# Cached keys of the differential attention loaded in 32 by 32 blocks and transposed by VectorE

## The chip, the cores and the metric

One core of one Trainium2 chip runs the whole step as one launch. The metric is the device time of one execution in microseconds (us). The core has TensorE (matrix products and full transposes through an identity matrix), VectorE, ScalarE, GpSimd and SyncE (SP), which issues most of the DMAs; 16 DMA engines carry them.

## The reference

One step of an encoder layer for two groups of requests that share the weights: a prompt of 1024 rows, and 8 running streams of 16 new rows each with 1024 cached rows. The layer has three branches (a recurrence, a differential attention, an attention over memory), a merge and a feed-forward part, all in fp32. The change touches only the scores of the running streams against their cached keys in the differential attention, which has 8 heads; a row of a cached key holds two keys of 64 values:

```python
def _diff_attention(q, k, v, pos_q, pos_k, rel_bias, lam):
    B, H, Lk, _ = k.shape
    k = k.reshape(B, H, Lk, 2, DIFF_DH)
    logits = jnp.einsum('bhqmd,bhkmd->bhmqk', q, k).astype(jnp.float32) * DIFF_SCALE
    logits = logits + _t5_bias(rel_bias, pos_q, pos_k)[None, :, None]
    p = jax.nn.softmax(jnp.where(visible, logits, -jnp.inf), axis=-1)
    w = p[:, :, 0] - lam * p[:, :, 1]
    return jnp.einsum('bhqk,bhkv->bhqv', w.astype(v.dtype), v)
```

`k` and `v` of a stream are the 1024 cached rows followed by its 16 new ones.

## The kernel before

The kernel runs phase by phase; `diff_phase` is the third. It loops over the heads, and each engine has its own instruction stream (`head(i)` in each block). A head has two parts. The prompt part goes over 8 blocks of 128 queries: scores `S0` to `S7`, their maximum on VectorE (`row_max`), the exponential on ScalarE (`probs`), the difference of the two maps on VectorE (`join`, which writes the weights), and a transpose of the weights with the product by the values (`T0` to `T8`) on TensorE. The sample part takes the 8 streams in two groups of 4: their cached keys must stand with the features on the partitions (`KT0` to `KT7`), then come the scores `SL0`, `SL1`, the maximum (`sample_max`), the exponential (`sample_probs`), the transposed weights (`PT0`, `PT1`) and the product by the cached values (`OS0`, `OS1`).

The names in the list `R` are results in PSUM, in the order in which TensorE makes them. They go in turn to two halves of PSUM, so a result waits until the last but one has been read (`take`, `freed`); `wait_freed` makes an engine wait until a result has been read. Twelve of them carry a rider: a third of one of the four projections (q, k, v, gate) that the next head or the end of this head needs, 24 matmuls that stand ahead of the result's own work in the same `take`, read by ScalarE in `finish`. The three gate riders go into the buffer `gt` ("diff_gate"). The weights of the riders are loaded by SP two at a time into a double buffer, rounded by ScalarE (`round_w`, line 108) and reduced to their rest by GpSimd (line 113). In a head ScalarE rounds the value weights right after `T0`, for all heads but the last.

The keys of a stream are 1024 rows of 128 values. One DMA (line 866) brings them with 128 rows on the partitions, 8 pieces of 512 bytes each. TensorE transposes the 8 tiles (line 1230) into PSUM, and ScalarE (line 974, even streams) or VectorE (line 1097, odd streams) copies them into `pb`, the buffer that holds the prompt's probabilities before, one place for each of 4 streams. There are four landing buffers: three of `cached_k`, and as slot 3 the gate's buffer, free between the store of one head's gate and the first gate rider of the same head's sample part. `kslot` says which stream goes to which buffer and in which turn.

SP issues in order, on one queue: the last head's gate and y stores, four key loads, four value loads (line 869), the value and gate weights, the stores of new keys and values, the next q and k weights, the prompt bias, the key loads 4 to 7 as buffers come free, value loads 4 to 7 after `OS0`, and the sample bias.

Of the kernel before, what the change touches and what calls it, by code (L numbers as in the profile page):

```python
# [14 lines left out]
P = 128  # L15
# [716 lines left out]
def diff_phase(g):  # L732
# [37 lines left out]
        "diff_consts_in", "bias_row_out", "bias_in", "bias_tables_ready", "bias_tables_out", "lambda_products",  # L770
        "lambda_exp", "diff_zeroed", "pool_turn"))

    kslot = ((0, 0), (1, 0), (3, 0), (2, 0), (0, 1), (1, 1), (2, 1), (0, 2))
    kbuf = [kc[:, 0], kc[:, 1], kc[:, 2], gt[:, 0:PAST].rearrange("p (t n) -> p t n", n=P)]
    kuses = [sum(n == slot for n, _ in kslot) for slot in range(len(kbuf))]
    kc_in, vc_in = [g.sem(f"cached_k{n}_in") for n in range(len(kbuf))], [g.sem(f"cached_v{n}_in") for n in range(4)]
    hbp_in, hbs_in = g.sem("head_bias_prompt_in"), g.sem("head_bias_sample_in")
    out_k, out_v, out_y, out_gt = (g.sem(n) for n in ("diff_k_out", "diff_v_out", "y1_out", "diff_gate_out"))
    (over_r, nm_r, w_r, sq_r, ln_r, rs_r, y_r, gt_r) = (g.sem(n) for n in (
# [5 lines left out]
    before = Results(g, ["Q", "BR", "K", "V"])  # L785
    g.r += before.n
    R = Results(g, ["S0", "VT", "S1", "KR", "S2", "T0", "S3", "T1", "S4", "T2", "S5", "T3", "S6", "T4", "S7", "T5",
                    "T6", "T7", "KT0", "T8", "KT1", "KT2", "KT3", "SL0", "KT4", "KT5", "KT6", "KT7", "PT0", "SL1",
                    "OS0", "PT1", "G", "OS1", "OC", "MS"])
    assert R.n % 2 == 0  # L790

    riders = dict(zip(("VT", "KR", "T0", "T1", "T2", "T3", "T4", "T5", "T6", "KT4", "G", "MS"),
                      [(p, c) for p in range(4) for c in range(NC)]))
    Q_LAST, K_LAST = "T0", "T3"

# [2 lines left out]
        return n in riders and not (last and riders[n][0] < 3)  # L798

    def bank(n):  # L800
        return 3 if n in ("VT", "KR", "MS") else 2

    def keys(t):

# [5 lines left out]
    with nc.Block() as block:  # L810
        @block.sync
        def _(sp):
# [47 lines left out]
            def load_k(i, b):  # L860
                slot, turn = kslot[b]
                if turn:
                    sp.wait_ge(g.full, R.full_value(f"KT{kslot.index((slot, turn - 1))}", i))
                if slot == 3:
                    sp.wait_ge(out_gt, i * 16 + 16)
                sp.dma_start(kbuf[slot], cached(kd, i, b)).then_inc(kc_in[slot], 16)

            def load_v(i, b):
                sp.dma_start(vc[:, b % 4], cached(vd, i, b)).then_inc(vc_in[b % 4], 16)
# [48 lines left out]
        def _(act):  # L918
# [11 lines left out]
            def head(i, last=False):  # L930
                def result(n):
                    return R.ready(act, n, i)

                def rider_out(n):

                    p, c = riders[n]

                    buf, scale = ((qn, DH ** -0.5), (kn, 1.0), (vt, 1.0), (gt, 1.0))[p]
                    if n == "T4":
                        act.wait_ge(out_k, i * 32 + 64)  # L940
                    elif n == "KT4":
                        act.wait_ge(out_gt, i * 16 + 16)
                    ins = act.activation(buf[:, c * CW:(c + 1) * CW], R.ready(act, n, i)[:, bank(n), 0:CW],
                                         ACT.Copy, scale=scale)
                    return ins
# [23 lines left out]
                        ins = act.activation(ot[:, (t - 1) * P:t * P], ps[:, 3, 0:P], ACT.Copy)  # L969
                    finish(f"T{t}", ins)  # L970

                def cached_kt(b):
                    ps = result(f"KT{b}")
                    finish(f"KT{b}", act.activation(pb[:, b % 4, 0:PAST], flat(ps[:, 0:2, :]), ACT.Copy))

                def sample_probs(n):
                    ps = flat(result(f"SL{n}"))
                    act.wait_ge(nm_r, i * 10 + (NQ + n + 1))
# [2 lines left out]

                def sample_turned(n):
                    ps = result(f"PT{n}")
                    R.freed(act.activation(tiles(wt[:, n, :]), ps[:, 0:NC, 0:CW], ACT.Copy), f"PT{n}")
                probs(0)
                ps = result("VT")
                act.wait_ge(out_v, i * 32 + 32)
# [11 lines left out]
                if not last:  # L999
                    g.round_w(act, first + 4, i, NW)  # L1000
                turned(NQ - 1)
                cached_kt(0)
                turned(NQ)
                cached_kt(2)
                act.wait_ge(y_r, i + 1)
                R.wait_freed(act, "T8", i)
                act.activation(sq[:, 0:SEQ], ot[:, 0:SEQ], ACT.Square)
                sample_probs(0)
                cached_kt(4)
                cached_kt(6)  # L1010
                sample_turned(0)
                sample_probs(1)
                sample_turned(1)
# [20 lines left out]
        def _(dve):  # L1034
# [33 lines left out]
            def head(i):  # L1068
                def result(n):
                    return R.ready(dve, n, i)  # L1070

                def row_max(t):
                    ps = result(f"S{t}").rearrange("p (m a) n -> p m (a n)", m=2)
                    near = slice(max(t - 1, 0) * P, keys(t))
                    w = near.stop - near.start
                    bias = hbp[:, 2 * P - w:2 * P].unsqueeze(1).to_broadcast([P, 2, w])
                    if t == 0:
                        dve.wait_ge(hbp_in, i * 16 + 16)
                    g.dve.done(dve.tensor_tensor(ps[:, :, near], ps[:, :, near], bias, ALU.add))
                    g.dve.done(dve.tensor_reduce(nm[:, t % 2, :], ps[:, :, 0:keys(t)], AX.X, ALU.max))  # L1080
                    dve.tensor_scalar(nm[:, t % 2, :], nm[:, t % 2, :], -1.0, None, ALU.mult).then_inc(nm_r, 1)

                def join(t):

                    a, b = pb[:, 2 * (t % 2), 0:keys(t)], pb[:, 2 * (t % 2) + 1, 0:keys(t)]
                    R.wait_freed(dve, f"S{t}", i)
                    g.dve.done(dve.reciprocal(cf[:, t % 2, :], sm[:, t % 2, :]))
                    g.dve.done(dve.tensor_scalar(cf[:, t % 2, 1:2], cf[:, t % 2, 1:2], nlam[:], None, ALU.mult))
                    g.dve.done(dve.tensor_scalar(a, a, cf[:, t % 2, 0:1], None, ALU.mult))
                    if t >= 2:  # L1090
                        dve.wait_ge(g.full, R.full_value(f"T{t - 2}", i))
                    dve.scalar_tensor_tensor(wb[:, t % 2, 0:keys(t)], b, cf[:, t % 2, 1:2], a, ALU.mult, ALU.add)\
                        .then_inc(w_r, 1)

                def cached_kt(b):
                    ps = result(f"KT{b}")
                    R.freed(dve.tensor_copy(pb[:, b % 4, 0:PAST], flat(ps[:, 0:2, :])), f"KT{b}")

                def sample_max(n):
                    ps = flat(result(f"SL{n}"))  # L1100
                    near = ps[:, PAST - P:ROWS]
                    g.dve.done(dve.tensor_tensor(near, near, hbs[:, n, :], ALU.add))
                    g.dve.done(dve.tensor_reduce(nm[:, n, 0:1], ps[:, 0:ROWS], AX.X, ALU.max))
                    dve.tensor_scalar(nm[:, n, 0:1], nm[:, n, 0:1], -1.0, None, ALU.mult).then_inc(nm_r, 1)

                def sample_factor(n):
                    R.wait_freed(dve, f"SL{n}", i)
                    g.dve.done(dve.reciprocal(cf[:, n, 0:1], sm[:, n, 0:1]))
                    g.dve.done(dve.tensor_tensor(cf[:, n, 0:1], cf[:, n, 0:1], sgn[:], ALU.mult))

                def sample_rows(n):

                    ps = result(f"OS{n}")
                    R.freed(dve.tensor_scalar(orow[:, n, :], ps[:, 0, 0:P], cf[:, n, 0:1], None, ALU.mult), f"OS{n}")
                row_max(0)
                row_max(1)
                for t in range(NQ):
                    join(t)
                    if t < NQ - 2:
                        row_max(t + 2)  # L1120
                cached_kt(1)
                cached_kt(3)
                dve.wait_ge(hbs_in, i * 16 + 16)
                sample_max(0)
                cached_kt(5)
                sample_factor(0)
                cached_kt(7)
                sample_max(1)
                sample_rows(0)
                sample_factor(1)  # L1130
                sample_rows(1)
                dve.wait_ge(rs_r, i + 1)
                dve.scalar_tensor_tensor(ot[:], ot[:], subl[:], sq[:], ALU.mult, ALU.mult).then_inc(y_r, 1)
# [45 lines left out]
        def _(pe):  # L1179
# [9 lines left out]
            def head(i, last=False):  # L1189
# [32 lines left out]
                                            stop=(n == t - 1))  # L1222
                    ins.then_inc(g.full, 1)

                def cached_kt(b):
                    ps, _ = take(f"KT{b}")
                    slot, turn = kslot[b]
                    pe.wait_ge(kc_in[slot], i * (16 * kuses[slot]) + 16 * (turn + 1))
                    for n in range(PAST // P):
                        ins = pe.transpose(ps[:, n // 4, (n % 4) * P:(n % 4 + 1) * P], kbuf[slot][:, n, :], g.ident[:])  # L1230
                    ins.then_inc(g.full, 1)

                def sample_scores(n):
                    ps, _ = take(f"SL{n}")
                    for b in (0, 1, 2, 3):
                        R.wait_freed(pe, f"KT{4 * n + b}", i)
                        rows = slice(b * 32, (b + 1) * 32)
                        for a in range(2):
                            pe.matmul(ps[rows, a, :], qb[:, 4 * n + b, :], pb[:, b, a * 512:(a + 1) * 512],
# [29 lines left out]
                    turn(t - 2)  # L1269
                turn(NQ - 2)  # L1270
                turn(NQ - 1)
                cached_kt(0)
                turn(NQ)
                for b in range(1, 4):
                    cached_kt(b)
                sample_scores(0)
                for b in range(4, DEC_B):
                    cached_kt(b)
                sample_turn(0)
                sample_scores(1)  # L1280
                sample_out(0)
# [1164 lines left out]
```

## Time and profile before

| | us |
|---|---|
| median of 3 runs | 3757.93 (3755.12 to 3761.45) |
| profiled execution, from first to last instruction (its span) | 3746.6 |
| TensorE matmuls busy | 3425.0 (91%) |
| VectorE busy | 1326.0 (35%) |
| ScalarE busy | 1170.4 (31%) |
| the DMA queue of SP, share of the 16 engines | 26.4% |

The profile gives the span of the profiled execution and no other time of it; the runs are timed with what lies before the first and after the last instruction, and their median is 11.3 us above the span. A wait is put down to what released it last. Times in the rows are counted from the start of the span.

### The profile page before, as it was taken

The numbers are of one execution on the slowest core, as the hardware profiler recorded it, in microseconds if no ns is written. First come the engines' busy times: TensorE is split into PE (matmuls) and PEld (weight loads), VectorE is DVE, ScalarE is ACT, GpSimd is POOL, SyncE is SP. The second block draws the span as 40 slices with busy tenths as digits, with TensorE's granted clock in tenths as the row PEclk, the third lists the DMA queues.
The fourth block names the chain that finished last, engine by engine and source line by source line (L and its number), as shares of the span: only waits on it lengthen the run. The fifth ranks groups of instructions, "written<-read, shape, count | busy, mean of one in ns | idle before, by whom it ended". The sixth has DMA issues, their size and how long they took to land. (4 is left out here: it accounts for less than half of the span.)

```text
span 3746.6 us, 51117 instructions
## 1 busy us (share of the span) xinstructions
PE 3425.0 (91%) x20480; PEld 3145.2 (84%) x20480; DVE 1326.0 (35%) x1424; ACT 1170.4 (31%) x1585; POOL 892.0 (24%) x522
## 2 busy tenths in 40 slices
PE   6999999999868999889968998899989999999997
PEld 5988899888857777777758887899988988888986
DVE  6344443453142343333431212122214443343443
ACT  4323333234223434433433222111223222222222
POOL 3233322332210111111101111124334222222220
PEclk8999999999989999999979998899989999999998
DMA  3111111011254244442444332543212111111101
GB/s 103 54 34 59 52 59 59 29 59 53 58 149 135 69 115 122 123 117 74 116 113 139 103 99 91 193 139 103 72 46 64 38 39 44 37 37 39 39 22 61
DMA packets 425088, 295.58 MB, mean 79 GB/s; under 512 B 17140, under 2 KB 405780, under 8 KB 425024
## 3 DMA queue, kind: packets, MB, share of 16 engines
q1 hardware_dynamic: 421616, 287.45, 26.4%
q10 hardware_dynamic: 3408, 7.22, 0.5%
q8 instruction: 47, 0.77, 0.1%
q14 instruction: 17, 0.14, 0.0%
HBM read 240.23 MB, written 54.41 MB: 79 GB/s over the span
## 5 line engine op out<-in xcount | busy, mean ns | idle before, releaser
L113 POOL TENSOR_TENSOR weight_lo<-weight_stage,weight_hi 128x1024 fp32r<-128x1024 f32 x180 | 436.1, 2423 | 1930.2 <-ACT weight_hi L108 1930.2
L160 PE MATMUL group<-h_hi_part,weight_hi 128*128 128x384 f32 x1608 | 581.2, 361 | 118.7 <-DVE key_rows L569 61.6
L161 PE MATMUL group<-h_lo_part,weight_hi 128*128 128x384 f32 x1608 | 558.4, 347 | 0.0
L162 PE MATMUL group<-h_hi_part,weight_lo 128*128 128x384 f32 x1608 | 557.5, 347 | 0.0
L160 PEld LDWEIGHTS group<-h_hi_part,weight_hi 128*128 128x128 f32 x1608 | 317.2, 197 | 155.5 <-issue 64.5
L1652 PE MATMUL group<-act_hi_part,weight_hi 128*128 128x512 f32 (+1 forms) x1056 | 378.0, 358 | 13.5 <-DVE act_lo_part L1880 9.1
L1654 PE MATMUL group<-act_hi_part,weight_lo 128*128 128x512 f32 (+1 forms) x1056 | 376.5, 357 | 0.0
L1653 PE MATMUL group<-act_lo_part,weight_hi 128*128 128x512 f32 (+1 forms) x1056 | 373.8, 354 | 0.0
L108 ACT ACTIVATE weight_hi<-weight_stage 128x1024 fp32r<-128x1024 f32 x180 | 190.7, 1060 | 497.4 <-PE group L1922 231.9
L161 PEld LDWEIGHTS group<-h_lo_part,weight_hi 128*128 128x128 f32 x1608 | 316.5, 197 | 1.9 <-issue 1.9
L162 PEld LDWEIGHTS group<-h_hi_part,weight_lo 128*128 128x128 f32 x1608 | 315.8, 196 | 0.0
L1920 PE MATMUL group<-act_hi_part,weight_hi 128*128 128x384 f32 x768 | 260.0, 339 | 11.3 <-DVE act_lo_part L1833 11.3
L1921 PE MATMUL group<-act_lo_part,weight_hi 128*128 128x384 f32 x768 | 259.0, 337 | 0.0
L1922 PE MATMUL group<-act_hi_part,weight_lo 128*128 128x384 f32 x768 | 259.0, 337 | 0.0
L1652 PEld LDWEIGHTS group<-act_hi_part,weight_hi 128*128 128x128 f32 x1056 | 200.2, 190 | 45.5 <-issue 9.7
L1654 PEld LDWEIGHTS group<-act_hi_part,weight_lo 128*128 128x128 f32 x1056 | 201.6, 191 | 32.8
L1653 PEld LDWEIGHTS group<-act_lo_part,weight_hi 128*128 128x128 f32 x1056 | 200.7, 190 | 32.6
L2168 DVE TENSOR_TENSOR residual<-residual,group 128x1152 f32<-128x1152 f32 x88 | 119.2, 1354 | 194.6 <-PE group L2257 194.6
L2255 PE MATMUL group<-ffn_hi_part,down_hi 128*128 128x384 f32 x528 | 178.9, 339 | 5.9 <-DVE ffn_lo_part L2163 5.9
L145 PE MATMUL group<-h_hi_part,weight_hi 128*128 128x384 f32 x504 | 173.9, 345 | 6.1 <-PEq L217 5.6
L2256 PE MATMUL group<-ffn_lo_part,down_hi 128*128 128x384 f32 x528 | 178.1, 337 | 0.0
L2257 PE MATMUL group<-ffn_hi_part,down_lo 128*128 128x384 f32 x528 | 178.0, 337 | 0.0
(328 smaller groups left out, 6160.7 us busy)
## 6 DMA issues: line engine op xcount, KB each, us to landing
weight_stage<-in_w_in SPq DMA_DIRECT2D x88, 512.0 KB, 4.1
cached_v<-in_cache_diff_v SPq DMA_DIRECT2D x64, 512.0 KB, 7.2
cached_k<-in_cache_diff_k SPq DMA_DIRECT2D x56, 512.0 KB, 4.1
weight_stage<-in_w_up SPq DMA_DIRECT2D x44, 512.0 KB, 3.7
y_stage<-scratch_y_branch SPq DMA_DIRECT2D x24, 576.0 KB, 9.8
gate_in<-scratch_gates SPq DMA_DIRECT2D x24, 576.0 KB, 3.7
weight_stage<-in_w_branch SPq DMA_DIRECT2D x24, 512.0 KB, 3.8
down_stage<-in_w_down SPq DMA_DIRECT2D x22, 512.0 KB, 3.6
```

The costliest lines, as they stand in the source:

```text
L108: act.activation(self.whi[:, n % 2, :], self.wst[:, n % 2, :], ACT.Copy).then_inc(self.w_hi, 1)
L113: pool.tensor_tensor(self.wlo[:, n % 2, :], self.wst[:, n % 2, :], self.whi[:, n % 2, :].bitcast(F32), ALU.subtract).then_inc(self.w_lo, 1)
L160: pe.matmul(out, wh[:, k, :], xh[:, k, cols], start=(k == 0), stop=False)
L161: pe.matmul(out, wh[:, k, :], xl[:, k, cols], start=False, stop=False)
L162: last = pe.matmul(out, wl[:, k, :], xh[:, k, cols], start=False, stop=(k == KT - 1))
L1652: pe.matmul(o, w[0][:, k, :], ahi[:, k, rows], start=(k == 0), stop=False)
L1653: pe.matmul(o, w[0][:, k, :], alo[:, k, rows], start=False, stop=False)
L1654: last = pe.matmul(o, w[1][:, k, :], ahi[:, k, rows], start=False, stop=(k == KT - 1))
L1920: pe.matmul(o, wh[:, k, :], ahi[:, k, cols], start=(k == 0 and open_sum), stop=False)
L1921: pe.matmul(o, wh[:, k, :], alo[:, k, cols], start=False, stop=False)
L1922: last = pe.matmul(o, wl[:, k, :], ahi[:, k, cols], start=False, stop=(k == KT - 1))
L2255: pe.matmul(o, dhi[:, f, cols], fhi[:, f, rows], start=(f == 0), stop=False)
```

## The change

The four landing buffers are used flat, as 128 by 1024. A stream's keys come in four DMAs, one for each 32 features: partition 32q + r gets, for each of 32 groups j of 32 rows, the 32 values 32q to 32q + 31 of row 32j + r. One instruction of VectorE then transposes all blocks of 32 by 32 and writes the keys into `pb`. The eight results `KT0` to `KT7`, their transposes on TensorE and their copies are gone, and the semaphore `cached_k_turned` takes their place for TensorE and SP. Stream 0 now uses slot 3, the gate's buffer. The rider that stood on `KT4` stands on `PT0`. VectorE turns streams 0 to 3 after the last `join` and streams 4 to 7 after the maximum of `SL0`.

```diff
-    kslot = ((0, 0), (1, 0), (3, 0), (2, 0), (0, 1), (1, 1), (2, 1), (0, 2))
-    kbuf = [kc[:, 0], kc[:, 1], kc[:, 2], gt[:, 0:PAST].rearrange("p (t n) -> p t n", n=P)]
+    kslot = ((3, 0), (0, 0), (1, 0), (2, 0), (0, 1), (1, 1), (2, 1), (0, 2))
+    kbuf = [flat(kc[:, 0]), flat(kc[:, 1]), flat(kc[:, 2]), gt[:, 0:PAST]]
...
-                    "T6", "T7", "KT0", "T8", "KT1", "KT2", "KT3", "SL0", "KT4", "KT5", "KT6", "KT7", "PT0", "SL1",
-                    "OS0", "PT1", "G", "OS1", "OC", "MS"])
+                    "T6", "T7", "T8", "SL0", "PT0", "SL1", "OS0", "PT1", "G", "OS1", "OC", "MS"])
...
@@ SP
             def load_k(i, b):
                 slot, turn = kslot[b]
                 if turn:
-                    sp.wait_ge(g.full, R.full_value(f"KT{kslot.index((slot, turn - 1))}", i))
+                    sp.wait_ge(kt_r, i * DEC_B + (kslot.index((slot, turn - 1)) + 1))
                 if slot == 3:
                     sp.wait_ge(out_gt, i * 16 + 16)
-                sp.dma_start(kbuf[slot], cached(kd, i, b)).then_inc(kc_in[slot], 16)
+                blocks = kd[b, ds(i, 1)].rearrange("h (j r) d -> r (h j) d", r=32)
+                for q in range(P // 32):
+                    sp.dma_start(kbuf[slot][q * 32:(q + 1) * 32, :].rearrange("r (j c) -> r j c", c=32),
+                                 blocks[:, :, q * 32:(q + 1) * 32]).then_inc(kc_in[slot], 16)
@@ ScalarE: the copies of KT0, KT2, KT4, KT6 go, and the gate rider waits for stream 0's transpose
-                    elif n == "KT4":
+                    elif n == "PT0":
                         act.wait_ge(out_gt, i * 16 + 16)
+                        act.wait_ge(kt_r, i * DEC_B + 1)
@@ VectorE
                 def cached_kt(b):
-                    ps = result(f"KT{b}")
-                    R.freed(dve.tensor_copy(pb[:, b % 4, 0:PAST], flat(ps[:, 0:2, :])), f"KT{b}")
+                    slot, turn = kslot[b]
+                    dve.wait_ge(kc_in[slot], i * (64 * kuses[slot]) + 64 * (turn + 1))
+                    if b < 4:
+                        dve.wait_ge(w_r, i * NQ + (NQ - 1 + b // 2))
+                    else:
+                        dve.wait_ge(g.full, R.full_value("SL0", i))
+                    dve.transpose(pb[:, b % 4, 0:PAST], kbuf[slot]).then_inc(kt_r, 1)
...
-                cached_kt(1)
-                cached_kt(3)
+                for b in range(4):
+                    cached_kt(b)
                 dve.wait_ge(hbs_in, i * 16 + 16)
                 sample_max(0)
-                cached_kt(5)
+                for b in range(4, DEC_B):
+                    cached_kt(b)
                 sample_factor(0)
-                cached_kt(7)
                 sample_max(1)
@@ TensorE: cached_kt and its calls go
                     for b in (0, 1, 2, 3):
-                        R.wait_freed(pe, f"KT{4 * n + b}", i)
+                        pe.wait_ge(kt_r, i * DEC_B + (4 * n + b + 1))
```

## Rows read from the trace of the kernel before

**Rows 1.** The page: the span, TensorE's total, the key loads (last column: landing).
```profile
span 3746.6 us, 51117 instructions
PE 3425.0 (91%) x20480; PEld 3145.2 (84%) x20480; DVE 1326.0 (35%) x1424; ACT 1170.4 (31%) x1585; POOL 892.0 (24%) x522
...
cached_k<-in_cache_diff_k SPq DMA_DIRECT2D x56, 512.0 KB, 4.1
```

**Rows 2.** TensorE's waits, 1060 to 2015 us: for whom, total, times, longest.
```profile
PE group L1206 <- ACT probs L957: 53.2, 20, 9.5
PE group L1230 <- DMA cached_k<-in_cache_diff_k: 12.3, 8, 1.7
```

**Rows 3.** What the weight rounding (line 108) waited for, 1060 to 2015 us.
```profile
  DMA weight_stage<-in_w_in: 35.1, 7
```

**Rows 4.** ScalarE's timeline: start, duration, instruction, [idle before it, releaser]; two heads.
```profile
1085.29 1.06 ACT L108 ACTIVATE weight_hi<-weight_stage 128x1024 fp32r<-128x1024 f32 x1 [12.18 <-DMA weight_stage<-in_w_in]
1101.22 0.91 ACT L957 ACTIVATE probs<-group,row_max 128x768 f32<-128x768 f32 x1 [3.28 <-DVE row_max L1081]
...
1446.69 1.06 ACT L108 ACTIVATE weight_hi<-weight_stage 128x1024 fp32r<-128x1024 f32 x1 [2.98 <-DMA weight_stage<-in_w_in]
1460.07 0.91 ACT L957 ACTIVATE probs<-group,row_max 128x768 f32<-128x768 f32 x1 [3.28 <-DVE row_max L1081]
```

**Rows 5.** TensorE's timeline: scores S4 of head 0, S1 and S4 of the other head.
```profile
1087.74 2.51 PE L1206 MATMUL group<-diff_k,diff_q 64*128 64x512 f32 x8 [9.46 <-ACT probs L957]
...
1427.38 0.84 PE L1206 MATMUL group<-diff_k,diff_q 64*128 64x256 f32 x4 [2.53 <-ACT probs L957]
...
1449.14 1.36 PE L1206 MATMUL group<-diff_k,diff_q 64*128 64x512 f32 x8 [0.26 <-ACT probs L957]
```

**Rows 6.** SP's timeline at the start of one head's loads.
```profile
1425.38 0.37 SPq L901 DMA_DIRECT2D scratch_gates<-diff_gate  x1
...
1427.00 1.88 SPq L866 DMA_DIRECT2D cached_k<-in_cache_diff_k  x2
...
1439.52 3.48 SPq L102 DMA_DIRECT2D weight_stage<-in_w_in  x2
```

**Rows 7.** The DMA view, 1430 to 1450 us: packets, bytes, rate.
```profile
DMA packets 11891, 5.99 MB, mean 300 GB/s; under 512 B 187, under 2 KB 11891, under 8 KB 11891
```

**Rows 8.** The DMA view, 4 to 5 us: loads of single fp32 values.
```profile
DMA packets 2152, 0.05 MB, mean 47 GB/s; under 512 B 2076, under 2 KB 2152, under 8 KB 2152
```

**Rows 9.** The DMA view, 1038 to 1041 us: bias loads into 16 partitions each.
```profile
DMA packets 1337, 0.32 MB, mean 108 GB/s; under 512 B 786, under 2 KB 1337, under 8 KB 1337
```

**Rows 10.** Windows: length, busy time of the five engines, granted clock, DMA share, GB/s.
```profile
1430.00:1432.00 2.00, 2.00 (x8) 2.00 (x7) 0.85 (x3) 0.95 (x4) 0.00 (x0) 0.50 1.15 327
```

**Rows 11.** VectorE's timeline in the same head: last `join`, first sample maximum.
```profile
1478.90 0.76 DVE L1089 TENSOR_SCALAR probs<-probs,row_factor 128x1024 f32<-128x1024 f32 x1
1479.88 1.28 DVE L1092 SCALAR_TENSOR_TENSOR weights<-probs,row_factor 128x1024 f32<-128x1024 f32 x1 [0.22 <-DVE probs L1089]
...
1498.32 0.43 DVE L1102 TENSOR_TENSOR group<-group,head_bias_sample 128x256 f32<-128x256 f32 x1 [2.42 <-PE group L1241]
```

**Rows 12.** TensorE's timeline, T8 (1489.34), SL0 (1494.58), KT4 to KT7, SL1 (1509.75).
```profile
1489.34 2.02 PE L1221 MATMUL group<-weights_t,diff_v_rows 128*128 128x128 f32 x16 [0.50 <-ACT diff_out L969]
...
1494.58 3.29 PE L1239 MATMUL group<-probs,query_blocks 128*32 128x512 f32 x16
1497.80 0.49 PE L1241 MATMUL group<-diff_k,query_blocks 128*128 128x128 f32 x2
1502.29 1.91 PE L1230 MATMUL group<-ident,cached_k 128*128 128x128 f32 x16
...
1509.75 1.95 PE L1239 MATMUL group<-probs,query_blocks 128*32 128x512 f32 x16 [0.34 <-DVE probs L1097]
1511.63 0.49 PE L1241 MATMUL group<-diff_k,query_blocks 128*128 128x128 f32 x2
```

**Rows 13.** ScalarE's timeline, the exponential of SL0.
```profile
1500.37 1.23 ACT L979 ACTIVATE weights<-group,row_max 128x1152 f32<-128x1152 f32 x1 [5.26 <-DVE row_max L1104]
```

More of the change, by code:

```diff
@@ L771, in diff_phase @@
         "lambda_exp", "diff_zeroed", "pool_turn"))
-    kslot = ((0, 0), (1, 0), (3, 0), (2, 0), (0, 1), (1, 1), (2, 1), (0, 2))
-    kbuf = [kc[:, 0], kc[:, 1], kc[:, 2], gt[:, 0:PAST].rearrange("p (t n) -> p t n", n=P)]
+    kslot = ((3, 0), (0, 0), (1, 0), (2, 0), (0, 1), (1, 1), (2, 1), (0, 2))
+    kbuf = [flat(kc[:, 0]), flat(kc[:, 1]), flat(kc[:, 2]), gt[:, 0:PAST]]
     kuses = [sum(n == slot for n, _ in kslot) for slot in range(len(kbuf))]
     kc_in, vc_in = [g.sem(f"cached_k{n}_in") for n in range(len(kbuf))], [g.sem(f"cached_v{n}_in") for n in range(4)]
+    kt_r = g.sem("cached_k_turned")
     hbp_in, hbs_in = g.sem("head_bias_prompt_in"), g.sem("head_bias_sample_in")
@@ L787, in diff_phase @@
     R = Results(g, ["S0", "VT", "S1", "KR", "S2", "T0", "S3", "T1", "S4", "T2", "S5", "T3", "S6", "T4", "S7", "T5",
-                    "T6", "T7", "KT0", "T8", "KT1", "KT2", "KT3", "SL0", "KT4", "KT5", "KT6", "KT7", "PT0", "SL1",
-                    "OS0", "PT1", "G", "OS1", "OC", "MS"])
+                    "T6", "T7", "T8", "SL0", "PT0", "SL1", "OS0", "PT1", "G", "OS1", "OC", "MS"])
     assert R.n % 2 == 0
-    riders = dict(zip(("VT", "KR", "T0", "T1", "T2", "T3", "T4", "T5", "T6", "KT4", "G", "MS"),
+    riders = dict(zip(("VT", "KR", "T0", "T1", "T2", "T3", "T4", "T5", "T6", "PT0", "G", "MS"),
                       [(p, c) for p in range(4) for c in range(NC)]))
@@ L800, in bank @@
     def bank(n):
-        return 3 if n in ("VT", "KR", "MS") else 2
+        return 3 if n in ("VT", "KR", "PT0", "MS") else 2
     def keys(t):
@@ L970, in turned @@
                     finish(f"T{t}", ins)
-                def cached_kt(b):
-                    ps = result(f"KT{b}")
-                    finish(f"KT{b}", act.activation(pb[:, b % 4, 0:PAST], flat(ps[:, 0:2, :]), ACT.Copy))
                 def sample_probs(n):
@@ L983, in sample_turned @@
                     ps = result(f"PT{n}")
-                    R.freed(act.activation(tiles(wt[:, n, :]), ps[:, 0:NC, 0:CW], ACT.Copy), f"PT{n}")
+                    finish(f"PT{n}", act.activation(tiles(wt[:, n, :]), ps[:, 0:NC, 0:CW], ACT.Copy))
                 probs(0)
@@ L1001, in head @@
                 turned(NQ - 1)
-                cached_kt(0)
                 turned(NQ)
-                cached_kt(2)
                 act.wait_ge(y_r, i + 1)
@@ L1008, in head @@
                 sample_probs(0)
-                cached_kt(4)
-                cached_kt(6)
                 sample_turned(0)
@@ L1095, in cached_kt @@
                 def cached_kt(b):
-                    ps = result(f"KT{b}")
-                    R.freed(dve.tensor_copy(pb[:, b % 4, 0:PAST], flat(ps[:, 0:2, :])), f"KT{b}")
+                    slot, turn = kslot[b]
[5 more added lines that the diff above has]
+                    dve.transpose(pb[:, b % 4, 0:PAST], kbuf[slot]).then_inc(kt_r, 1)
                 def sample_max(n):
@@ L1223, in turn @@
                     ins.then_inc(g.full, 1)
[L1225 to L1231, printed above, removed]
                 def sample_scores(n):
@@ L1271, in head @@
                 turn(NQ - 1)
-                cached_kt(0)
                 turn(NQ)
-                for b in range(1, 4):
-                    cached_kt(b)
                 sample_scores(0)
-                for b in range(4, DEC_B):
-                    cached_kt(b)
                 sample_turn(0)
```

## The prediction

> **What bounds the kernel now.** I read the totals first, then who waits for whom in the stage of the change, then one head by engine, then the DMA queue. TensorE is busy for 91% of the span [rows 1], so an instruction taken off it counts almost in full, unless the time goes into a wait. The eight heads of the differential attention lie between about 1060 and 2015 us, near 119 us each; the head shown begins its loads at 1427.00 and ends its sample part near 1530. Two waits of TensorE matter in them: for ScalarE's `probs` (53.2 us in 20 waits) and for the cached keys (12.3 us in 8) [rows 2].
>
> The first has a cause one step further back. In seven heads ScalarE rounds the next value weights right after T0, and stands still for their landing: 35.1 us in 7 waits [rows 3]; 12.18 us in head 0, 2.98 us in the head shown [rows 4]. TensorE then waits for the `probs` behind that rounding: 9.46 us in head 0, 0.26 us in the head shown [rows 5], so 2.7 us of delay are covered and every further one reaches TensorE in full. What it waits for is a queue: SP issues the gate and y stores, four key loads, four value loads, then the weights at 1439.52 [rows 6], and from 1430 to 1450 the DMA engines never rest (300 GB/s [rows 7], a busy share of 1.15 in its first 2 us [rows 10]). **Whatever makes the four key loads longer makes each of these seven waits longer**, one for one. The landing is on the path already.
>
> **The loads.** Per head, 8 key loads of 1024 packets of 512 B become 8 groups of four DMAs with 4096 packets of 128 B in all; the bytes stay. 11891 packets in 20 us are 16 x 20000 / 11891 = 26.9 ns for one packet on one engine, 64 of them 1.72 us a load; by bytes (512 KB at 300 GB/s) 1.75 us, which I use [rows 7]. No row has 128 B packets. Below lies the column load of 4 B packets: 2076 in 1 us, 7.7 ns each [rows 8]; above, 26.9 ns if a packet of 128 B costs what one of 512 B does. A straight line between them gives 7.7 + 124/508 x 19.2 = 12.4 ns, and 256 x 12.4 = 3.2 us a load. The new DMAs write 32 partitions each. Where the kernel loads its bias with DMAs into 16 partitions, the queue moved 0.32 MB in 3 us, 108 GB/s [rows 9]; if that is a limit of the partitions, 32 have twice as much, 2.4 us a load. I take 3.4 us, the line and a little for the crowding; the ends are 2.0 (7.7 ns) and 6.9 us (26.9 ns).
>
> The Trainium skill, page "DMA: Bandwidth & Descriptors", section "Why small descriptors are slow (HBM only)", puts a fixed cost of about 3 cycles on each packet beside one for every 32 B. That would make a 128 B packet cost 7/19 of a 512 B one, an estimate of 10.1 ns and 2.6 us a load; by the sum below that is 3749 us, a little faster than now.
>
> Four loads of a head stand before the weights: 4 x (3.4 - 1.75) = 6.6 us. The first load of a head now goes to slot 3, the gate's buffer, and waits for the gate store; the first load was issued at 1427.00 and this one can go about 1428.3 (the store issued at 1425.38, some 2.9 us to landing), but the y store still fills the engines then, so I put 0.5 us (0 to 1.3) on it. SP issues 12 more instructions for the four loads at 0.35 to 0.4 us, inside the time of the transfers. So the weights land 7.1 us later in seven heads: 50 us. The last head rounds nothing after T0 and pays nothing.
>
> A long wait also costs TensorE its clock. After 9.46 us of waiting in head 0, ScalarE's `probs` of 768 keys came 1101.22 - 1085.29 = 15.9 us behind the rounding's start, against 1460.07 - 1446.69 = 13.4 us in the head shown [rows 4]: 2.5 us. In the head shown TensorE waits 2.53 us at 1427.38 [rows 5], and from 1430 to 1432 the granted clock is 0.50, the lower of its two levels (1.2 and 2.4 GHz) [rows 10]. Six heads now join head 0: 15 us. Cost in front: 65 us.
>
> **The tail of a head.** Gone from TensorE are 64 transposes a head in groups of 8 at about 1.04 us, 8.3 us, with the waits between them. ScalarE and VectorE lose four PSUM copies each. VectorE gains eight transposes of 128 x 1024. Not in the trace; the nearest rows of that length are 0.76 us (probs scaled in SBUF) and 1.28 us (the join of two) [rows 11]; I take 1.25 us, and 2.5 us as the worse end. The first four start when the last join ends, at 1481.2, and take until 1486.2, or 1491.2 at the worse end; T8 ends at 1491.4 [rows 12], so they are covered either way. Their price if they were not is 1.25 us each.
>
> The two sample scores decide. SL0 could start at 1494.58, and stretched to 3.29 us waiting for the copy of key 3; now it starts at 1491.4, runs 1.95 us as SL1 does, and with its last matmuls is done at 1493.8, not 1498.3 [rows 12]. From there TensorE must wait, because the gate product that filled this gap rides on PT0 behind the exponentials: VectorE's maximum takes from 1498.32 to 1500.2 and ScalarE's exponential 1.23 us and a read [rows 11, 13], so TensorE idles 3.5 us, to 1497.3. The product takes 4.1 us (1498.2 to 1502.3 before), PT0's transposes 1.15: 1502.5. SL1 needs the eighth key, whose buffer is free only when key 4 is transposed: 1493.8 + 1.9 + 1.25 = 1497.0. Its load took 4.1 us to land [rows 1], now 4.1 + 1.65 = 5.75, so 1502.9, transposed 1504.2, and SL1 ends at 1505.2 against 1512.1: 6.9 us earlier. All waits of the keys are in that. If the clock falls in the 3.5 us of idling, the product takes some 2.7 us more and SL1 ends at 1507.6: 4.5 us. The half clock of rows 10 came after a gap of 2.53 us, other gaps went without, so I give this an even chance and take 5.5 us; eight heads give 44 us.
>
> **Sum.** +50 +15 -44 = +21 us. On the span of 3746.6 us this is 3768; the runs' median is 11.3 us above the span (stretches before and after it that the change leaves alone), so 3757.9 + 21 = **3779 us**, 0.6% slower. Every 0.1 us a load moves it by 2.8 us.
>
> **Rivals.** A, faster: the small packets are cheap, at the partition bound of 2.4 us a load. The wait in front grows by 4 x 0.65 + 0.5 = 3.1 us, 22 us in seven heads, 8 for the clock, and the tail gives 48: 3740, and 3730 to 3750 around it. It decides below about 2.65 us a load. For it: 4 B packets pass at 7.7 ns, so little of a packet's cost needs to be fixed. Against: between the two sizes that the trace shows, the line asks for more. The skill's estimate above falls to this side.
>
> B, no change: 2.65 to 2.85 us a load, 3751 to 3765; the two terms then cancel.
>
> C, much slower: a 128 B packet costs nearly what a 512 B one does, 5 to 6.9 us. At 6.9 the landing is 21 us late in seven heads (148 us), 15 us for the clock, and keys 4 to 6, requested near 1484, are in at 1506, so the eighth lands at 1513 and the tail loses 3 us a head instead of gaining: 3945. At 5 us it is 3835 to 3840. For it: no row has such packets from HBM into SBUF in number. The Trainium skill, same page, "Specifications", says that below 512 B a transfer is no longer at line rate, since a read-modify-write is done; the 4 B row does not bear out a heavy price.
>
> D, VectorE's transposes take 2.5 us or more: SL1 comes 2.5 us later, 20 us in all on top of the forecast, 3799. It decides only once eight of them no longer fit the 10 us before SL0. Against: a pass over 1024 values takes 1.28 us.
>
> **Chances.** Forecast (2.85 to 4.2 us a load, D's case with it) 0.50, its own range 3765 to 3805; A 0.22, B 0.13, C 0.15. The range that leaves out 2 in 10 cuts the far end of C and the lowest of A: 3738 to 3850. This kernel's measurement tells about 0.2% (7.5 us) from no change; below 3750.4 lies A, within it B: faster 0.22, same 0.13, slower 0.65.
>
> **What would show it.** ScalarE's wait for the weights: from 35 us in seven heads to about 85; 35 to 60 speaks for A or B, over 130 for C. TensorE's wait for `probs` grows with it. The granted clock of the stretch behind T1 falls to 0.50 in all seven heads. The DMA window of the head's start shows packets of 128 B at 12 to 14 ns. VectorE's transpose row reads near 1.25 us, and its wait for key 7 is the last before SL1. I am wrong if the packets' cost is off by more than 0.8 us a load, or if the sample part ends no earlier.

## The result, and the profile after

The changed kernel took 3770.09 us (median of 4 runs, 3767.17 to 3774.05) against 3756.52 us before (4 runs, 3751.8 to 3761.45): ratio 1.004, 95% interval 1.0025 to 1.0054. The change costs 0.4%; 3779 us was forecast. The profiled execution has a span of 3765.2 us, 18.6 us above that of before. That is more than the 13.6 us between the medians. The section on the time before put the 11.3 us between median and span down to what lies before and after the instructions; the changed kernel's executions show only 1.9 to 3.0 us of that (3767.17 us for the span of 3765.2). So the profiled execution of before was itself some 8 us faster than its median.

The page after, then TensorE's waits in the stage (for whom, total, times, longest) and ScalarE's waits at the rounding; [rows 1 to 3] have them before:

```profile
span 3765.2 us, 50542 instructions
PE 3381.5 (90%) x19968; PEld 3113.5 (83%) x19968; DVE 1362.1 (36%) x1456; ACT 1139.0 (30%) x1553; POOL 892.7 (24%) x522
...
cached_k<-in_cache_diff_k SPq DMA_DIRECT2D x224, 128.0 KB, 4.2
```

```profile
PE group L1207 <- ACT probs L961: 104.6, 20, 16.0
PE group L160 <- ACT weights L979: 28.2, 8, 3.5
PE group L1222 <- ACT diff_out L973: 10.3, 8, 1.4
```

```profile
  DMA weight_stage<-in_w_in: 88.1, 7
```

TensorE is busy 43.5 us less and the kernel is slower: the saved work went into waits. ScalarE stands 88.1 us for the weights instead of 35.1, and TensorE 104.6 us for the `probs` behind it instead of 53.2 [rows 2, 3]. Two heads in ScalarE's timeline, and TensorE's scores S4 behind the rounding ([rows 4, 5] before):

```profile
1091.21 1.06 ACT L108 ACTIVATE weight_hi<-weight_stage 128x1024 fp32r<-128x1024 f32 x1 [18.68 <-DMA weight_stage<-in_w_in]
...
1214.05 1.06 ACT L108 ACTIVATE weight_hi<-weight_stage 128x1024 fp32r<-128x1024 f32 x1 [12.05 <-DMA weight_stage<-in_w_in]
```

```profile
1093.65 2.51 PE L1207 MATMUL group<-diff_k,diff_q 64*128 64x512 f32 x8 [15.96 <-ACT probs L961]
1216.49 2.51 PE L1207 MATMUL group<-diff_k,diff_q 64*128 64x512 f32 x8 [9.33 <-ACT probs L961]
```

Over the seven heads TensorE's waits at S4 add up to 69.0 us, against 16.1 before: +53.0 us. The DMA view during the key loads of heads 1 and 2:

```profile
DMA packets 12107, 1.53 MB, mean 139 GB/s; under 512 B 12107, under 2 KB 12107, under 8 KB 12107
...
DMA packets 13730, 1.74 MB, mean 145 GB/s; under 512 B 13706, under 2 KB 13730, under 8 KB 13730
```

The first is 1192 to 1203 us, 16 x 11000 / 12107 = 14.5 ns for one 128 B packet on one engine; the second 1314 to 1326 us, 14.0 ns. A load so takes 3.6 to 3.7 us where it took 1.75.

The tail of head 1 on TensorE (T8, SL0, the gate product from 1265.97, PT0, SL1, the first matmuls of OS0), and on VectorE ([rows 11, 12] before):

```profile
1258.10 2.05 PE L1222 MATMUL group<-weights_t,diff_v_rows 128*128 128x128 f32 x16 [1.28 <-ACT diff_out L973]
1260.08 1.94 PE L1232 MATMUL group<-probs,query_blocks 128*32 128x512 f32 x16
1261.96 0.49 PE L1234 MATMUL group<-diff_k,query_blocks 128*128 128x128 f32 x2
1265.97 0.44 PE L160 MATMUL group<-h_hi_part,weight_hi 128*128 128x384 f32 x1 [3.52 <-ACT weights L979]
1271.83 1.15 PE L179 MATMUL group<-ident,weights 128*128 128x128 f32 x9
1272.90 1.95 PE L1232 MATMUL group<-probs,query_blocks 128*32 128x512 f32 x16
1274.78 0.49 PE L1234 MATMUL group<-diff_k,query_blocks 128*128 128x128 f32 x2
```

```profile
1249.94 1.24 DVE L1098 STREAM_TRANSPOSE probs<-diff_gate 128x1024 f32<-128x1024 f32 x1
1251.10 3.46 DVE L1098 STREAM_TRANSPOSE probs<-cached_k 128x1024 f32<-128x1024 f32 x3
...
1264.51 3.50 DVE L1098 STREAM_TRANSPOSE probs<-cached_k 128x1024 f32<-128x1024 f32 x3
1271.21 1.25 DVE L1098 STREAM_TRANSPOSE probs<-cached_k 128x1024 f32<-128x1024 f32 x1 [3.20 <-DMA cached_k<-in_cache_diff_k]
```

SL0 comes right behind T8 and takes 1.94 us, TensorE idles 3.52 us in all eight heads (28.2 us above), and the gate product takes 5.86 us (1265.97 to 1271.83) where it took 4.25 (1498.04 to 1502.29), since the clock falls within it: its matmuls take 0.34 us each, from 1267.75 to 1270.63 0.52, and 0.34 again. In six heads it takes 5.8 to 5.9 us, in the other two 6.67 and 7.08. The windows (length, five engines' busy time, granted clock, DMA share, GB/s) of the stretch behind S4 and of the gate product both show 0.50, the lower of the two levels. The third line is the stretch behind S4 of the same head before. Behind S4 the clock is 0.50 in all seven heads after, in head 0 alone before.

```profile
1216.00:1219.00 3.00, 2.51 (x9) 1.27 (x9) 0.00 (x0) 1.26 (x5) 1.53 (x1) 0.50 0.80 239
...
1268.00:1270.00 2.00, 2.00 (x8) 2.00 (x8) 0.01 (x1) 0.00 (x0) 0.00 (x0) 0.50 1.28 172
...
1210.00:1213.00 3.00, 2.47 (x16) 1.70 (x15) 0.72 (x2) 1.60 (x7) 1.87 (x1) 1.00 1.05 318
```

What the lower clock costs shows from the start of S4 to the product of T7, which holds the same work in both kernels. T7's product in head 1 after, then in the head shown before (S4 at 1216.49 and 1449.14):

```profile
1254.99 1.83 PE L1222 MATMUL group<-weights_t,diff_v_rows 128*128 128x128 f32 x14 [0.69 <-ACT next_v L947]
...
1486.14 1.83 PE L1221 MATMUL group<-weights_t,diff_v_rows 128*128 128x128 f32 x14 [0.68 <-ACT next_v L943]
```

That is 38.5 us against 37.0. Over the seven heads it adds up to 272.2 us after and 261.5 before: +10.7 us.

From T8 to the first product of OS0 it is 17.3 us here, 22.9 in the head shown before (1489.34 to 1512.27). Summed over the eight heads, 141.8 us against 184.3: -42.5 us. So the 18.6 us of the two spans are +53.0 at the weights, +10.7 from S4 to T7, -42.5 in the tails, -6.8 in the rest of the stage (3.7 of it in the last head before T8) and +4.2 behind the stage, in code that is the same. No run shows a cause for the last term; it is about as large as the 5.0 us by which the spans differ more than the medians.

### The profile page after: what moved, and what is told of

Its sections match the earlier page's. It is cut to its first block and busy times, and to the rows that moved or that the text cites. A ratio compares the mean times of both kernels' runs of the same rounds, so it can differ in the third digit from the quotient of the medians.

```text
span 3765.2 us, 50542 instructions
## 1 busy us (share of the span) xinstructions
PE 3381.5 (90%) x19968; PEld 3113.5 (83%) x19968; DVE 1362.1 (36%) x1456; ACT 1139.0 (30%) x1553; POOL 892.7 (24%) x522
## 5 line engine op out<-in xcount | busy, mean ns | idle before, releaser
L160 PE MATMUL group<-h_hi_part,weight_hi 128*128 128x384 f32 x1608 | 590.8, 367 | 147.4 <-DVE key_rows L569 61.6
L161 PE MATMUL group<-h_lo_part,weight_hi 128*128 128x384 f32 x1608 | 567.1, 353 | 0.0
L162 PE MATMUL group<-h_hi_part,weight_lo 128*128 128x384 f32 x1608 | 566.4, 352 | 0.0
L1640 PE MATMUL group<-act_hi_part,weight_hi 128*128 128x512 f32 (+1 forms) x1056 | 378.5, 358 | 13.5 <-DVE act_lo_part L1868 9.1
L1207 PE MATMUL group<-diff_k,diff_q 64*128 64x512 f32 (+3 forms) x384 | 93.0, 595 | 106.2 <-ACT probs L961 106.2
L145 PE MATMUL group<-h_hi_part,weight_hi 128*128 128x384 f32 x504 | 174.5, 346 | 6.1 <-PEq L217 5.6
```

Of the source, the lines that this page charges most:

```text
L160: pe.matmul(out, wh[:, k, :], xh[:, k, cols], start=(k == 0), stop=False)
L161: pe.matmul(out, wh[:, k, :], xl[:, k, cols], start=False, stop=False)
L162: last = pe.matmul(out, wl[:, k, :], xh[:, k, cols], start=False, stop=(k == KT - 1))
L1640: pe.matmul(o, w[0][:, k, :], ahi[:, k, rows], start=(k == 0), stop=False)
```

## The experiments

The kernel before was run beside each group of experiments; its medians were 3753.35 us (e1 to e4), 3751.86 (e5 to e8) and 3750.69 (e9 to e11). So kernels are compared by their ratio to it, where the changed kernel has 1.004.

### e1 and e2: the weights issued ahead of the keys

The same move in both kernels:

```diff
+                g.load_w(sp, following[0], first + 2, i, NW)
+                if not last:
+                    g.load_w(sp, following[1], first + 3, i, NW)
                 for b in range(4):
                     load_k(i, b)
                 for b in range(4):
                     load_v(i, b)
-                g.load_w(sp, following[0], first + 2, i, NW)
-                if not last:
-                    g.load_w(sp, following[1], first + 3, i, NW)
```

> The changed kernel with one move on SP: the value and gate weights are issued before the four key loads of a head, not behind the value loads. My theory (the key packets cost time only because the weights stand behind them in the queue): ScalarE's 88 us of waits for the weights go, TensorE's waits behind the rounding (15.96 us in head 0, near 9 us in six heads, about 70 us) go, and with them 7 x 2.5 us of low clock: 3770 - 87 = 3683 us. The first four keys land 3.5 us later and stay covered. Rival (the seven waits are not the price; the loss is spread, in contention of the DMA engines or in the tail): less than half of it comes back, over 3725 us.

> The kernel before with the same move. My theory: its 35 us of waits for the weights hold 16 us of waits of TensorE and one fall of the clock (2.5 us): 3756 - 18 = 3738 us. With e1 this shows what the change is worth once the queue is out of the way: about 55 us. Rival (the gate product's new gap and the clock eat the saved transposes): e1 is no better than e2.

e1: 3681.38 us (3678.48 to 3688.88), ratio 0.9811 (0.9788 to 0.9834), 2.3% below the changed kernel, some 86 us; 87 were expected. ScalarE waits for weights no more, and S4 to T7 adds up to 259.0 us, so the waits are worth 69.0 us and the clock 13.2. e2: 3731.05 us (3730.25 to 3734.72), ratio 0.9944 (0.9924 to 0.9963), 22 us below the kernel before; 18 were expected. TensorE's two longest waits in the stage, in e1, then in e2:

```profile
PE group L1207 <- ACT probs L961: 35.9, 13, 6.9
PE group L160 <- ACT weights L979: 28.2, 8, 3.5
```

```profile
PE group L1206 <- ACT probs L957: 36.2, 13, 6.9
PE group L1230 <- DMA cached_k<-in_cache_diff_k: 12.2, 8, 1.6
```

The waits for `probs` are now equal, 13 in place of 20: the seven at S4 are gone in both. So in the changed kernel the key packets cost time through the queue in front of the weights, and with that out of the way the change is worth 1.3% (0.9811 against 0.9944), about 50 us. Once the weights go first, the packets show in the tail too (e8). The rival that the new gap eats the saved transposes falls.

### e3: the changed kernel with rows of 512 B

```diff
-                blocks = kd[b, ds(i, 1)].rearrange("h (j r) d -> r (h j) d", r=32)
-                for q in range(P // 32):
-                    sp.dma_start(kbuf[slot][q * 32:(q + 1) * 32, :].rearrange("r (j c) -> r j c", c=32),
-                                 blocks[:, :, q * 32:(q + 1) * 32]).then_inc(kc_in[slot], 16)
+                sp.dma_start(kbuf[slot].rearrange("p (t n) -> p t n", n=P), cached(kd, i, b)).then_inc(kc_in[slot], 64)
```

> The changed kernel with each key load as one DMA of rows of 512 B, as before; VectorE transposes what is there, so the scores of the cached keys are of wrongly arranged keys. My theory: the waits for the weights fall from 88 back to about 35 us, and the saving of the tail stays (5.5 us a head, and key 7 lands 1.5 us earlier): 3700 to 3712 us. Rival (the four transposes more on VectorE, or slot 3 first, hold part of the loss): it stays above 3730 us.

3708.24 us (3704.46 to 3713.27), ratio 0.9885 (0.9865 to 0.9905). ScalarE's waits at the rounding are back at what they were in [rows 3]:

```profile
  DMA weight_stage<-in_w_in: 36.3, 7
```

VectorE transposes keys that are wrongly arranged here, so this is a probe and no kernel to use. All else of the change is in, and it is 45 us faster than before. The gain of the tail is real, and the whole loss is in how the keys are fetched.

### e4: the kernel before with 128 B packets

TensorE's wait for the keys counts four DMAs here (not shown):

```diff
-                sp.dma_start(kbuf[slot], cached(kd, i, b)).then_inc(kc_in[slot], 16)
+                for q in range(P // 32):
+                    cols = slice(q * 32, (q + 1) * 32)
+                    sp.dma_start(kbuf[slot][:, :, cols], cached(kd, i, b)[:, :, cols]).then_inc(kc_in[slot], 16)
```

> The kernel before with each key load cut into four DMAs of 32 features, over all 128 partitions: 128 B packets, and all else as it was. My theory (a packet of 128 B costs 14 ns whatever the partitions): each load takes 3.6 us instead of 1.75, the weights land 7.5 us later in seven heads (53 us), 15 us of clock, and key 7 lands 1.9 us later in eight heads (15 us): 3756 + 83 = 3839 us. Rival (the 32 partitions of one DMA are what made the loads long, the packets alone take 2.6 us): 3756 + 24 + 10 + 7 = 3797 us or less.

3833.72 us (3829.33 to 3838.12), ratio 1.0211 (1.0189 to 1.0233): 80 us slower, 83 expected. The waits at the rounding, and the DMA view from 1069 to 1078 us (14.6 ns a packet):

```profile
  DMA weight_stage<-in_w_in: 84.1, 7
```

```profile
DMA packets 9861, 1.26 MB, mean 140 GB/s; under 512 B 9860, under 2 KB 9860, under 8 KB 9860
```

Packets of 128 B alone, with TensorE still transposing, bring the waits. The waits at S4 grow from 16.1 to 65.0 us, S4 to T7 from 261.5 to 274.6, and the tails from 184.3 to 200.2: 78 of the 80 us. Here each DMA goes to all 128 partitions, so the packet price does not come from the 32.

### e5 and e6: packet size and number of partitions, taken apart

Both leave the keys wrongly arranged for the block transposes. e5 writes 128 B packets over 128 partitions, e6 packets of 512 B into 32. Each replaces the four lines of the change that issue the DMAs (not shown):

```diff
 e5
+                rows = kbuf[slot].rearrange("p (t n) -> p t n", n=P)
+                for q in range(P // 32):
+                    cols = slice(q * 32, (q + 1) * 32)
+                    sp.dma_start(rows[:, :, cols], cached(kd, i, b)[:, :, cols]).then_inc(kc_in[slot], 16)
 e6
+                    part = slice(q * 32, (q + 1) * 32)
+                    sp.dma_start(rows[part], cached(kd, i, b)[part]).then_inc(kc_in[slot], 16)
```

> The changed kernel with the same four DMAs of 128 B packets a load, but each over all 128 partitions (8 pieces of 128 B a partition) in place of 32 partitions (32 pieces); the keys are then wrongly arranged for the block transposes. Theory (packet size alone): no change, 3763 to 3776 us, 14 to 14.5 ns a packet. Rival (32 partitions crowd): packets near 10 to 12 ns and 3715 to 3750 us.

> The changed kernel with four DMAs of 32 partitions a load, but 512 B packets (8 a partition); keys wrongly arranged. Theory (packet size alone): as e3, 3703 to 3713 us. Rival (a DMA into 32 partitions moves at most 217 GB/s, 2.4 us a load): 4 x 0.65 us later in seven heads, 3725 to 3732 us.

e5: 3766.38 us (10 runs, 3757.28 to 3774.29), ratio 1.0035 (1.0025 to 1.0046), no different from the changed kernel. Its packets take 13.5 ns (1192 to 1200 us; 14.5 in the same stretch of the changed kernel), and its waits at the rounding are 80.5 us, 0.27 us a load less. e6: 3740.41 us (10 runs, 3736.06 to 3746.63), ratio 0.9971 (0.9959 to 0.9983): 32 us more than e3, which differs only in the number of partitions. Its DMA view is that of 1183 to 1190 us, a stretch of key loads; its waits at the rounding follow. First comes the DMA view of e5, 1192 to 1200 us.

```profile
DMA packets 9507, 1.20 MB, mean 150 GB/s; under 512 B 9507, under 2 KB 9507, under 8 KB 9507
```

```profile
DMA packets 2956, 1.42 MB, mean 203 GB/s; under 512 B 176, under 2 KB 2956, under 8 KB 2956
```

```profile
  DMA weight_stage<-in_w_in: 54.9, 7
```

At 512 B the 32 partitions do bind: 203 GB/s, near twice the 108 of [rows 9]. The landing is (54.9 - 36.3) / 7 = 2.7 us later, 0.67 us a load, which makes it 2.4 us, the figure that the prediction named as a bound. At 128 B the packet price is the larger one, and the partitions add about 1 ns to it. The 32 us of e6 are waits and clock: from e3 to e6 TensorE's waits at S4 grow from 17.3 to 35.7 us in seven heads, and S4 to T7 from 261.9 to 276.1, 14.2 us. The windows from 1190 to 1230 us, around S4 of head 1, show the granted clock at 1.00 in e3 and 0.91 in e6:

```profile
1190.00:1230.00 40.00, 38.68 (x225) 32.62 (x224) 22.47 (x37) 16.64 (x38) 7.49 (x3) 1.00 0.55 145
...
1190.00:1230.00 40.00, 35.05 (x187) 29.18 (x185) 17.84 (x33) 15.11 (x36) 4.73 (x2) 0.91 0.56 142
```

### e7 and e8: the tail

```diff
 e7
-                    R.wait_freed(pe, f"SL{n}", i)
                     ps, _ = take(f"PT{n}")
+                    R.wait_freed(pe, f"SL{n}", i)
 e8: e1 and e7, and
-    kslot = ((3, 0), (0, 0), (1, 0), (2, 0), (0, 1), (1, 1), (2, 1), (0, 2))
+    kslot = ((3, 0), (0, 0), (1, 0), (2, 0), (0, 1), (1, 1), (2, 1), (3, 1))
-                        act.wait_ge(kt_r, i * DEC_B + 1)
+                        act.wait_ge(kt_r, i * DEC_B + 8)
```

> The changed kernel with two lines of TensorE swapped: PT0 is taken, with its gate product, before the wait for the exponentials of SL0, so the product fills the 3.5 us of idling. Theory (key 7's landing is the last thing before SL1, its transpose ends 1.1 us before SL1 does): SL1 can end only 1.6 us earlier, 13 us in eight heads: 3757 us. Rival (TensorE's gap and its clock are the bound of the tail): the whole 3.5 us and the slow product's 1.8 us come back, 5 us a head: 3728 us.

> The changed kernel with the weights issued first (e1), PT0 taken first (e7), and key 7 loaded into slot 3 as its second turn, right after key 0 is transposed, where it no longer waits for key 4; ScalarE's gate rider waits for all eight transposes in return. Theory: e1's gain, and SL1 ends some 5 us earlier in each of eight heads: 3681 - 40 = 3641 us. Rival (the gate rider, which now waits for key 7, holds back OS0): 3665 us or more.

e7: 3766.66 us (3761.43 to 3772.02), ratio 1.0041 (1.0026 to 1.0055): nothing gained that these runs can tell, where 13 us were expected. The gate product is back at 4.25 us in all eight heads. TensorE's gap closed and opened again one step later, in SL1:

```profile
1269.23 2.45 PE L1232 MATMUL group<-probs,query_blocks 128*32 128x512 f32 x12
1274.47 1.90 PE L1232 MATMUL group<-probs,query_blocks 128*32 128x512 f32 x4 [2.79 <-DVE probs L1098]
```

Both bounds of the tail, key 7 and TensorE's own gap, lay within 0.5 us of each other (key 7 transposed at 1272.46 in the head shown after, SL1 started at 1272.90). And the last stream's four matmuls alone take 1.90 us, as long as all sixteen do when nothing holds them up, so starting SL1 early for three streams gives nothing.

e8: 3666.52 us (5 runs, 3661.47 to 3669.95), ratio 0.9774 (0.9756 to 0.9791), 2.3% below the kernel before and the fastest of all; but only 14 us below e1, where 40 were expected. In its head 1:

```profile
1236.91 2.44 PE L1232 MATMUL group<-probs,query_blocks 128*32 128x512 f32 x12
1240.40 1.90 PE L1232 MATMUL group<-probs,query_blocks 128*32 128x512 f32 x4 [1.05 <-DVE probs L1098]
```

```profile
1239.11 1.25 DVE L1098 STREAM_TRANSPOSE probs<-diff_gate 128x1024 f32<-128x1024 f32 x1 [1.71 <-DMA diff_gate<-in_cache_diff_k]
```

VectorE still waits for key 7, now not for its buffer but for its turn in the queue: SP issues its four DMAs at 1231.96, behind those of keys 4 to 6 at 3.7 us each. Small packets bound the tail as well. The time is the one that the rival had named (3665 us or more), but its mechanism is not seen: the gate rider does not hold OS0 back, whose first product follows SL1 without a wait in all eight heads.

### e9 and e10: the transposes doubled

```diff
+                    if b < 4:   # e10: b >= 4
+                        dve.transpose(pb[:, b % 4, 0:PAST], kbuf[slot]).then_inc(twice, 1)
+                        dve.wait_ge(twice, i * 4 + (b % 4 + 1))
                     dve.transpose(pb[:, b % 4, 0:PAST], kbuf[slot]).then_inc(kt_r, 1)
```

> The changed kernel with each of the first four transposes of a head done twice, the second after the first: 4.8 us more of VectorE's work a head. Theory (these four lie under TensorE's products of T7 and T8, with 3 us to spare): no change within 3 us of the changed kernel, 3767 to 3774 us. Rival D's condition met (they reach the path): 2 us or more a head, 3786 us or more.

> The changed kernel with each of the last four transposes of a head done twice. Theory (key 4's transpose stands before key 7's load, and key 7's transpose before SL1): 1.25 us twice a head on the path, 2.5 us, 20 us in all: 3790 us. Rival (TensorE's gap and the slow product are the bound of the tail): key 7 has slack, and less than 5 us in all is lost.

e9: 3775.68 us (3771.84 to 3789.31), ratio 1.0074 (1.0051 to 1.0097), above the changed kernel's 1.004 with intervals that just touch; no loss was expected. In head 1 SL0 was not held up: the doubled transposes end at 1261.6 and SL0 starts at 1262.05 behind T8, with no wait. The buffers came free later, so SP began keys 4 to 7 at 1256.98 (1252.47 in the changed kernel), and VectorE waited for two of them. SL1, 12.8 us behind SL0's start in the changed kernel, is 13.7 behind it here, but in this head not for the keys: the gate product took 6.70 us at the lower clock, PT0's transposes came behind it at 1274.63, and key 7 was ready at 1274.97, before they ended. VectorE, then TensorE:

```profile
1270.13 1.25 DVE L1102 STREAM_TRANSPOSE probs<-cached_k 128x1024 f32<-128x1024 f32 x1 [1.28 <-DMA cached_k<-in_cache_diff_k]
1273.72 1.25 DVE L1102 STREAM_TRANSPOSE probs<-cached_k 128x1024 f32<-128x1024 f32 x1 [2.35 <-DMA cached_k<-in_cache_diff_k]
...
1274.63 1.14 PE L179 MATMUL group<-ident,weights 128*128 128x128 f32 x9
1275.71 1.94 PE L1236 MATMUL group<-probs,query_blocks 128*32 128x512 f32 x16
```

In heads 0, 2, 5 and 7 key 7 was the later one, by 0.2 to 1.2 us. And in the last head SL0 itself was held up, its last four products starting when the doubled transposes end:

```profile
1989.08 1.93 PE L1236 MATMUL group<-probs,query_blocks 128*32 128x512 f32 x12
1991.35 1.90 PE L1236 MATMUL group<-probs,query_blocks 128*32 128x512 f32 x4 [0.34 <-DVE probs L1102]
```

Over the eight heads the tails are 145.3 us against 141.8, 3.6 us of the some 13. The rest lies outside the tails (the waits at S4 are 72.4 us against 69.0, S4 to T7 276.2 against 272.2), and no cause is shown for it. e10: 3786.38 us (3781.44 to 3790.88), ratio 1.0094 (1.0077 to 1.0111), 0.54% or 20 us above the changed kernel, as expected; its rival had under 5 us. From SL0's start to SL1's end it is 17.5 us in head 1 against 15.2, and the tails add up to 156.6 us against 141.8, so 15 of the 20 us are in them.

### e11: the order of the landing buffers

```diff
-    kslot = ((3, 0), (0, 0), (1, 0), (2, 0), (0, 1), (1, 1), (2, 1), (0, 2))
+    kslot = ((0, 0), (1, 0), (3, 0), (2, 0), (0, 1), (1, 1), (2, 1), (0, 2))
-                        act.wait_ge(kt_r, i * DEC_B + 1)
+                        act.wait_ge(kt_r, i * DEC_B + 3)
```

> The changed kernel with the landing buffers in the order of before (slot 3, which waits for the gate store, third and not first); ScalarE's gate rider waits for the third transpose in return. Theory (the y store fills the engines while the first load waits): under 0.5 us a head in front, 3766 to 3770 us. Rival (the first load's wait for the gate store costs its full 1.4 us): 10 us, 3760 us.

3772.55 us (3763.74 to 3776.43), ratio 1.0053 (1.0035 to 1.007): no difference from the changed kernel that these runs can tell. The waits for the weights are 85.7 us in place of 88.1, 0.3 us a head. The full 1.4 us a head is ruled out by that.

## Why the prediction held

The forecast was +21 us for the two terms in front and the one behind; the two executions differ by 18.6, the medians by 13.6. Queue, waits, clock and tail work as the prediction has them. That the sum of the two spans comes so close is in part luck: the terms give +53.0 +10.7 -42.5 = +21.2, and the -6.8 and +4.2 us beside them were not forecast. The step from span to median by 11.3 us was misread (see the result); as the forecast adds its difference to a measured median, it does no harm there.

**The packets.** 12.4 ns by the line between 4 B and 512 B, 3.4 us a load taken; measured 14.0 to 14.5 ns, 3.6 to 3.7 us. The crowding for the 32 partitions was put at 0.2 us a load and is 0.27 by e5; the rest is that 128 B packets lie above the line, by 1.1 ns over 128 partitions in e5. The rule of the Trainium skill ("DMA: Bandwidth & Descriptors", "Why small descriptors are slow (HBM only)") of about 3 cycles a packet gave an estimate of 10.1 ns, 30% below the measured price, and a small gain; the measurement decides against that estimate here. That under 512 B the line rate is lost (same page of the Trainium skill, "Specifications"), the trace bears out: 139 to 145 GB/s against 300.

**The weights.** 7.1 us later forecast, (88.1 - 35.1) / 7 = 7.6 measured; 50 us forecast, 53.0 at S4. e1 and e2 take this term out, e4 brings it into the kernel before, e3 removes it from the changed one. For slot 3 I had put 0.5 us; e11 says 0.3, a difference within what the executions vary by.

**The clock.** The prediction took 2.5 us for each of six heads from the one long wait of head 0, 15 us. From S4 to T7's product the six heads take 1.4 to 1.7 us more in four cases and 3.0 and 2.6 in two, 11.7 us; head 0, at the lower clock in both kernels, takes 1.1 us less. So the term is +10.7, about 30% under its forecast, in the profiled execution. In e5, e7, e9, e10 and e11, which leave this stretch as it is, the seven heads take 273.8 to 276.2 us, 12.3 to 14.7 above before: there the forecast was nearly met.

**The tail.** 44 us forecast, 42.5 measured. The transpose took 1.20 to 1.25 us (1.25 taken), TensorE's gap 3.52 us (3.5), SL0 1.94 us (1.95). The clock did fall behind that gap, to which an even chance had been given, and it fell in all eight heads. The forecast for that case alone was 4.5 us a head, 36 us, with 2.7 us for the slower product; it cost 1.6 us in six heads, 2.4 and 2.8 in two. That the mean of the two cases met the measured 5.3 us a head is luck. The other case also let SL1 end 1.0 us behind key 7's transpose, where its last four products alone take 1.90 us (e7). Rival D is out, by the row of the transpose and by e10, whose doubling cost what a transpose of 2.5 us was priced at (20 us). What the step missed: "covered either way" holds for SL0 in seven heads of e9 and not in the last, and it does not hold for the key buffers, whose release the first four transposes also time (e9).

**The rivals.** A and B needed under 2.85 us a load, C over 5. With e3 one sees what A would have been at its best: 512 B in place of 128 B turns a loss of 0.4% into a gain of 1.15%.

## What to carry to other kernels

Moving work off the busiest engine by asking the DMA for a finer layout is paid for in packets, and the price is collected by whatever stands behind those loads in the queue. Ask who that is before the change: here it was a weight load on the critical path, and issuing it first turned a loss of 0.4% into a gain of 1.9%. Two bounds that lie half a microsecond apart must both be moved, and the release of a landing buffer is worth a look as well as its first use.

## What the runs showed that I had not expected

DMAs of 512 B packets into 32 partitions ran at 203 GB/s against 290 to 300 into 128 (e6, e3), while with 128 B packets the number of partitions hardly mattered (14.0 to 14.5 ns against 13.5 to 14.6). Sixteen products of 32 columns for four streams take 1.94 us together, and the four of the last stream alone 1.90 us (e7, e8): the four streams' products overlap, and the last one to be ready costs the time of all. And the lower clock behind a wait of TensorE has no fixed price: 1.4 to 3.0 us a head from S4 to T7 behind waits of 7.8 to 16.0 us, with the same work in each head.
